# Sample attention: which engine copies the transposed keys out of PSUM, and where ScalarE stands its exponentials

## The reference, cut to what matters

```python
def masked_softmax(s, mask):
    s = jnp.where(mask, s.astype(jnp.float32), -1e30)
    p = jax.nn.softmax(s, axis=-1)
    return jnp.where(mask, p, 0.0)
...
def mem_attend(q, kv):
    ...
    s = jnp.einsum('bthd,bmhd->bhtm', q, kv[:, :, 0]) * MEM_SCALE
    p = jax.nn.softmax(s.astype(jnp.float32), axis=-1).astype(q.dtype)
    return jnp.einsum('bhtm,bmhd->bthd', p, kv[:, :, 1]).reshape(B, T, MEM_Q)
```

## Time and profile before

| | us |
|---|---|
| three runs | 1620.06, 1617.21, 1621.73 |
| their median | 1620.06 |
| profiled execution, first to last instruction | 1605.8 |
| median less the profiled span: what lies around it, and the profile's own deviation | 14.3 |
| TensorE busy in the span | 1432.8 (89%) |
| sample attention, first to last of its work | 779 to 913 |

### The profile page before, as it was taken

One profiled execution on the slowest core, in us unless ns is written; L12 is line 12 of the kernel. 1 busy time (PEld: TensorE's weight loads), 2 busy tenths in 40 slices (PEclk: granted clock), 3 DMA queues, 4 the chain that ended last, 5 costly groups with the idle time before them and its releaser, 6 DMA issues. The chain is left out here.

```text
span 1605.8 us, 27033 instructions
## 1 busy us (share of the span) xinstructions
PE 1432.8 (89%) x11344; PEld 1317.2 (82%) x11344; DVE 867.8 (54%) x1573; ACT 388.7 (24%) x892; POOL 82.0 (5%) x76
## 2 busy tenths in 40 slices
PE   6999899897978787979665699999899999999998
PEld 5788788897967685868443598999898999999998
DVE  3455165947744565555333546545738656455563
ACT  3544013221353444444222231000012101010000
POOL 1000001100001111111100000000000000000000
PEclk8999999998999897979687899999899999999999
DMA  9132035142421000010466532332331323232321
GB/s 357 63 125 106 1 109 185 57 168 79 141 55 53 1 2 0 2 53 1 167 239 242 208 95 78 114 99 82 111 125 54 106 79 106 80 104 78 105 80 54
DMA packets 115648, 159.03 MB, mean 99 GB/s; under 512 B 6039, under 2 KB 106839, under 8 KB 112778
## 3 DMA queue, kind: packets, MB, share of 16 engines
q1 hardware_dynamic: 111886, 122.76, 23.5%
q0 software_dynamic: 2304, 33.56, 5.2%
q10 hardware_dynamic: 1348, 1.12, 0.2%
HBM read 145.04 MB, written 16.66 MB: 101 GB/s over the span
## 5 line engine op out<-in xcount | busy, mean ns | idle before, releaser
L330 PE MATMUL ps<-uH,wh 128*128 128x260 f32 x576 | 165.3, 287 | 8.8 <-DVE wt L301 8.8
L330 PE MATMUL ps<-hH,wh 128*128 128x260 f32 x512 | 144.9, 283 | 2.6 <-DVE hT L301 2.6
L330 PE MATMUL ps<-mergedH,wh 128*128 128x260 f32 x512 | 145.7, 285 | 0.0
L330 PE MATMUL ps<-mergedT,wh 128*128 128x260 f32 x512 | 144.8, 283 | 0.0
L330 PE MATMUL ps<-hT,wh 128*128 128x260 f32 x512 | 144.8, 283 | 0.0
L330 PE MATMUL ps<-mergedH,wl 128*128 128x260 f32 x512 | 144.5, 282 | 0.0
L330 PE MATMUL ps<-hH,wl 128*128 128x260 f32 x512 | 144.5, 282 | 0.0
L457 PE MATMUL ps<-XT,w 128*128 128x256 f32 (+1 forms) x512 | 125.4, 386 | 6.3 <-DVE XT L520 6.0
L330 PEld LDWEIGHTS ps<-uH,wh 128*128 128x128 f32 x576 | 109.3, 190 | 14.1 <-DVE wt L301 9.0
L330 PE MATMUL ps<-uL,wh 128*128 128x260 f32 x384 | 108.5, 283 | 0.0
L330 PE MATMUL ps<-uH,tw 128*128 128x260 f32 x384 | 108.5, 283 | 0.0
(11 more groups left out here) (532 smaller groups left out, 3416.7 us busy)
## 6 DMA issues: line engine op xcount, KB each, us to landing
wt<-in_w_ff SPq DMA_DIRECT2D x32, 1024.0 KB, 5.2
wt<-in_w_in SPq DMA_DIRECT2D x15, 1024.0 KB, 5.6
tw<-in_w_in SPq DMA_DIRECT2D x12, 1024.0 KB, 5.2
ring<-in_cache_mem_kv SPq DMA_DIRECT2D x4, 2048.0 KB, 10.8
w<-in_cmp_w SPq DMA_DIRECT2D x8, 512.0 KB, 6.3
ring<-in_cache_win_kv SPq DMA_DIRECT2D x2, 2048.0 KB, 9.5
out_s_win<-in_cache_win_kv SPq DMA_DIRECT2D x1, 4088.0 KB
scratch_uhigh<-uH SPq DMA_DIRECT2D x1, 2080.0 KB
```

The lines of the kernel that those rows point to most:

```text
L330: ins = pe.matmul(out, lhsT(i, c), rhs(j, c), start=(first and c == 0 and k == 0), stop=(last and c == chunks - 1 and k == 2))
```

## The change

Two things are changed, both in the order of work only; the arithmetic is the same.

First, the engine of a unit comes from a table. All four key units of a win job go to ACT. Of a mem job's first four key units ACT has the first two and DVE the next two. All other units alternate as before. The waits on the two counters are rewritten so that they count the units of each engine by the table (`by(e, u)`).

Second, the exponentials of sel and win jobs get another number. Before they stood at 10n + 8.75 and up, ahead of the next job's key copies. Now sel's stand at 10(n + 1) + 0.8, behind all four key copies of the win job (10(n + 1) to 10(n + 1) + 0.75), and win's at 10(n + 1) + 0.3, behind the first two of the mem job's key copies. Those of mem stay.

```diff
-        own = lambda u: u % 2
+        own = {}
+        for n, (br, r) in enumerate(jobs):
+            for x in range(4 * GROUPS[br]):
+                own[key_units[n] + x] = 1 if br == "win" or (br == "mem" and x < 2) else 0 if br == "mem" and x < 4 else (key_units[n] + x) % 2
+            for x in range(NPROB(br) + (br != "mem")):
+                own[prob_units[n] + x] = (prob_units[n] + x) % 2
+        by = lambda e, u: sum(own[x] == e for x in range(u + 1))
...
         soft_key = lambda n, i: key(n, 8.0 + i / 4)
+        exp_key = lambda n, i: key(n + 1, (0.8 if jobs[n][0] == "sel" else 0.3) + i / 100)
...
                 if u >= 2:
-                    pe.wait_ge(kept[u % 2], u // 2)
+                    pe.wait_ge(kept[own[u - 2]], by(own[u - 2], u - 2))
...
-                pe.wait_ge(kept[0], (u + 1) // 2)
-                pe.wait_ge(kept[1], u // 2)
+                pe.wait_ge(kept[0], by(0, u - 1))
+                pe.wait_ge(kept[1], by(1, u - 1))
...
-                        if own(u) == mine:
+                        if own[u] == mine:
...
-                    yield soft_key(n, 3 + i)
+                    yield soft_key(n, 3 + i) if br == "mem" else exp_key(n, i)
```

## The result

| | before | changed |
|---|---|---|
| median, us | 1615.71 (15 runs, 1606.43 to 1621.73) | 1606.10 (15 runs, 1595.84 to 1611.34) |
| ratio to before | | 0.9941, 95% interval 0.9923 to 0.9959 |
| profiled execution: its span / time | 1605.8 / not listed | 1608.1 / 1609.84 |
| sample attention, first matmul to DVE's last product | 778.97 to 913.09: 134.12 | 789.14 to 915.32: 126.18 |

The kernel is faster by 0.6%: 9.5 us of 1615.71, with 6.6 to 12.4 in the interval. I had forecast 9.2. The profiled span of the changed kernel is longer than that of before: two spans cannot be compared as wholes here.

What follows compares the result with a forecast made beforehand. TensorE, busy 89%, could gain only where it stood waiting for copies and gathers. 5.0 + 5.0 + 0.9 - 1.7 = 9.2 us off the 1605.8 span, plus 14.3 around it: 1610.9 us; range 1606.5 to 1617.0.

Steps and rivals of the forecast that it cites:

- The copies and the exponentials: Win's key copies on ACT ahead of sel's exponentials: DVE's first copy of turned exponentials 5.0 us earlier per half.
- The next wait: After the change, DVE's wait for all four exponentials before newp and the reciprocal would be late next, until 816.64.
- The gathers: Sel 1's gathers start 5.0 us earlier and take the same time, so the first half's gain is all kept.
- The clock: One 3.4 us stretch of slow TensorE clock over solid work in the two halves, costing 1.7 us; bounds none and two.
- Mem's part: Mem's first two key units on ACT, next two on DVE: nothing in half 0, 0.9 us in half 1.
- the small store: Win 1's result store, issued earlier, meets the next stage's loads and lands about 905.5, giving half 1's 0.9 us.
- the base: The 1605.8 us span plus 14.3 us around it, matching the median of 1620.06, from which the gain was subtracted.
- less 1.5 for the spread of the runs: Allowance at the range's lower end, taken off 1608.0 us (no slow stretch, mem's gain in full).

Runs made afterwards that it cites:

- the fills: Changed kernel plus unread matmuls in the two short TensorE stalls around sel's first turned exponentials, in each half; 1603.59 us, ratio to before 0.9936.
- the win part's: Kernel before with only win's key copies on ACT and sel's exponentials behind them, mem's key units and win's exponential as before; 1604.54 us, ratio 0.9957.
- newp later: Changed kernel, but for sel DVE makes newp and the reciprocal behind its first copy of turned exponentials; 1603.86 us, ratio to before 0.9924.
- fill in the first: Changed kernel with 8 unread matmuls only between win's scores and sel's turned exponentials, none before the value product; 1599.87 us in one run.
- loads late: Changed kernel with SP's three loads of the next stage moved behind its wait for the small stores; 1620.40 us in one run.

## Why the prediction was right, and where it failed

**The copies and the exponentials** (5.0 in each half): 4.96 and 4.95. The next wait was where I had put it, DVE's wait for all four exponentials.

**The gathers** carry half 0's gain through: 23.44 us before, 23.76 after.

**The clock** (one slow stretch, 1.7): the number of stretches was wrong. There were two in both profiles of the changed kernel, and they cost 1.8 and 1.7 us. I had the row that said so, the fall of the clock after a stall of 2.36 us, and halved it without a reason. Either of the two short stalls was enough. Whether transposes keep the clock up less well than other matmuls was not tested; the fills are plain matmuls. The Trainium skill's rule on long idle gaps ("TensorE: Matmul & The Clock Gate", "Why this matters for your kernels") would have left no slow stretch; the trace disagrees, since no stall between win's keys and the value product was over 1.84 us and the clock fell.

**Mem's part** (0.9): 0.2 against the profile from which I worked, 1.4 against the second one of before, and through mem's last product. Through the small store, where I had looked for it, it was worth nothing.

Between the second profiles of both kernels these terms give 9.9 - 3.6 + 1.4 = 7.7, and the stage shrank by 7.66. Between the first ones they give 9.9 - 3.5 + 0.2 = 6.6, and the stage shrank by 7.94. The difference is in the first profile of before alone. It reached sel 0's maximum 31.90 us behind the stage's start, ahead of anything that was changed, and every other profile at 30.86 to 31.09; another 0.7 stands between the last gathered piece and sel 1's maximum, and the gathers give 0.3 back. The interval of 6.6 to 12.4 holds both. That my 9.2 lies so near to the 9.5 between the medians is partly luck: by the second profiles it was 1.5 too much: 1.9 for the clock, less 0.5 that mem's part brought beyond my 0.9.

**What failed is the base.** The sum's step "with the 14.3 us around it that is 1610.9 against the median of 1620.06" took three runs as the kernel's time, and the range's "less 1.5 for the spread of the runs" took their spread as its spread. Around a span there are 1.8 us. The rest of the 14.3 was the difference between a short execution (a span of 1605.8) and three longer ones. With 15 runs the median of before was 1615.71, and that of 31 further runs 1614.21 (1604.48 to 1620.19). The forecast of 1610.9 missed 1606.1 by 4.8 us: 4.35 are 1620.06 - 1615.71, the rest is 9.6 against 9.2. From 1615.71 my 9.2 would have given 1606.5. The spread of before's 15 runs is 15.3 us, where I allowed 1.5. Most of it is made ahead of the stage. The first 774 us of three profiles, the changed kernel's, before's and the win part's, which are the same program there:

```profile
0.00:774.00 774.00, 677.98 (x4919) 604.77 (x4920) 424.86 (x820) 277.77 (x650) 70.24 (x67) 0.91 0.24 81
```

```profile
0.00:774.00 774.00, 673.22 (x4982) 601.76 (x4982) 426.88 (x827) 281.22 (x655) 70.29 (x67) 0.93 0.23 81
```

```profile
0.00:774.00 774.00, 667.79 (x4982) 596.80 (x4982) 429.68 (x833) 280.89 (x655) 73.07 (x69) 0.94 0.24 81
```

The stage began the later, the lower the mean clock was up to there: at 789.1, 779.0 and 774.0 with 0.91, 0.93 and 0.94. Over all profiles it began between 774.0 and 789.1, while what follows the stage took 692.4 to 695.2. The timed runs fit: the shortest of the changed kernel's 15 (1595.84) had a mean clock of 0.949, the longest (1611.34) 0.936. Why the clock differs there from one execution to the next was not looked into.

## What to carry to other kernels

When an engine's list has copies that free a buffer behind work that waits for something long, give those copies to the engine that is idle then, and put them ahead of its own waiting work; here one half alone cost 3.8 us and the other brought 2.2, against 6.0 for both. Count what a removed stall leaves behind: short stalls in front of solid matmuls (1.84 us here) can still drop the clock, and the work behind them pays. And before a time is forecast from a few runs, ask how far one execution's span lies from them, and read a change of 0.5% from the stage it touches.

## What the runs showed of the hardware

TensorE's granted clock fell from its upper to its lower level behind one stall of 1.84 us (newp later, 815.1) and behind one of 1.94 us (fill in the first, 813.8), with no other idle stretch over 0.8 us since its last wait for a gathered piece. Unread matmuls in such stalls kept it up, and the value products took 5.8 us instead of 7.4 and 7.3.

A store of 64 KB on ACT's queue waited for large loads on SP's. Sel's store landed 10.1 us behind its issue with these loads on their way and 1.5 behind it with the loads late:

```profile
scratch_sel<-osb ACTq DMA_DIRECT2D x1, 64.0 KB, 1.5
```

SP was released 1.7 us behind the issue of win's store with the loads late and 4.7 behind it in the changed kernel.
